# A hybrid streaming encoder step: expert weights through one ring of fourteen half-size slots, with the residual kept on chip and the first projection reordered

## The reference, cut to what matters

```
x = x + gate * mixer(adaLN(rmsnorm(x), c))     # layer 0: GLA + gated DeltaNet heads, layer 1: MLA attention
x = x + gate * moe(adaLN(rmsnorm(x), c))       # both layers
moe(h): 4 groups x 8 experts = 32; a token takes the best group and its 2 best experts
        y = sum of 2 of  w * (silu(h @ w1[e]) * (h @ w3[e])) @ w2[e]     # 1024 -> 512 -> 1024
layer-0 mixer: z = h @ w_in (1024 x 3608); a short convolution, silu and l2norm on q, k; chunked scans; output product
y = rmsnorm(x)
```

## Time and profile before

| what | value |
|---|---|
| median of three runs | 2421.89 us (2415.78 to 2421.91) |
| the profiled execution | 2422.05 us, span of its instructions 2420.2 us |
| mean granted TensorE clock | 0.874 of full speed |
| busy: PE / DVE / ACT / POOL | 79% / 26% / 20% / 5% of the span |
| moved by DMA | 557.66 MB, mean 230 GB/s |
| projection of layer 0 | about 68 to 349 us |
| experts of layer 0 and of layer 1 (routing to last product) | 763 to 1321 us, 1803 to 2362 us |
| combine of layer 0 and of layer 1 | 1338 to 1367 us, 2378 us to the end |

### The profile page before, as it was taken

How to read it: one execution, slowest core, us unless ns; L and a number is a source line. 1 busy time by engine, 2 the same in 40 slices (tenths; PEclk the granted TensorE clock), 3 DMA queues, 4 the chain that set the end, 5 groups by cost and what they waited for, 6 DMA issues and landing times. The chain is left out here.

```text
span 2420.2 us, 29969 instructions
## 1 busy us (share of the span) xinstructions
PE 1900.4 (79%) x12405; PEld 1167.0 (48%) x12405; DVE 633.5 (26%) x1309; ACT 482.2 (20%) x905; POOL 124.3 (5%) x167
## 2 busy tenths in 40 slices
PE   4899937777494889889896189999956989898980
PEld 1899925667484433333332154566953333333420
DVE  1225326334545100100110512333442100010104
ACT  3232262211302000000000341344120000000003
POOL 0000000210000110000000000000001001010000
PEclk7889956798795899999999599999957999999995
DMA  7343380144525399999996720101351999999984
GB/s 292 70 158 132 132 56 5 66 155 144 204 98 187 139 428 385 428 414 401 399 395 284 275 72 3 68 1 36 133 216 60 425 410 406 414 401 405 399 350 176
DMA packets 130328, 557.66 MB, mean 230 GB/s; under 512 B 43432, under 2 KB 76024, under 8 KB 104336
## 3 DMA queue, kind: packets, MB, share of 16 engines
q1 hardware_dynamic: 116176, 535.63, 57.0%
q0 software_dynamic: 11520, 17.85, 2.1%
q10 hardware_dynamic: 2496, 2.23, 0.3%
HBM read 541.65 MB, written 38.12 MB: 240 GB/s over the span
## 5 line engine op out<-in xcount | busy, mean ns | idle before, releaser
L1948 PE MATMUL ex_p<-ring,ex_xT 128*64 128x512 f32 (+1 forms) x1024 | 472.3, 619 | 69.8 <-DMA second<-in_moe_w 67.1
L1948 PE MATMUL ex_p<-second,ex_xT 128*64 128x512 f32 (+1 forms) x1024 | 468.8, 615 | 0.0
L1948 PEld LDWEIGHTS ex_p<-ring,ex_xT 128*64 128x64 f32 (+1 forms) x1024 | 156.4, 156 | 368.0 <-issue 364.5
L2011 DVE TENSOR_TENSOR ex_gm<-ex_s,ex_p 128x512 f32<-128x512 f32 x40 | 27.5, 688 | 891.4 <-issue 859.8
L1964 PE MATMUL ex_py<-ring,ex_gT 128*64 128x512 f32 (+1 forms) x512 | 231.7, 606 | 33.5 <-DMA second<-in_moe_w 17.9
L1964 PE MATMUL ex_py<-second,ex_gT 128*64 128x512 f32 (+1 forms) x512 | 232.1, 607 | 6.3 <-DVE ex_gT L2015 6.3
L1948 PEld LDWEIGHTS ex_p<-second,ex_xT 128*64 128x64 f32 (+1 forms) x1024 | 155.7, 155 | 61.2 <-issue 61.2
L1995 ACT COPY ex_y<-ex_py 128x1024 f32<-128x1024 f32 x40 | 40.5, 1012 | 707.0 <-PE ex_py L1964 707.0
L1964 PEld LDWEIGHTS ex_py<-ring,ex_gT 128*64 128x64 f32 (+1 forms) x512 | 75.4, 152 | 161.2 <-issue 132.8
L230 PE MATMUL ab_z<-ab_hh,ab_wh 128*128 128x288 f32 (+3 forms) x272 | 79.9, 294 | 25.9 <-DVE ab_wl L264 25.9
L230 PE MATMUL out_py<-out_wh,out_oh 128*128 128x256 f32 (+1 forms) x320 | 92.3, 289 | 1.9 <-DVE out_ol L1575 1.8
(11 more groups left out here) (426 smaller groups left out, 3037.2 us busy)
## 6 DMA issues: line engine op xcount, KB each, us to landing
ring<-in_moe_w SPq DMA_DIRECT2D x96, 2048.0 KB, 16.0
second<-in_moe_w SPq DMA_DIRECT2D x96, 2048.0 KB, 18.1
ring<-in_ada_w SPq DMA_DIRECT2D x32, 1536.0 KB, 7.9
ring<-in_ab_w_in SPq DMA_DIRECT2D x7, 2048.0 KB, 7.7
cb_y<-yrow SPq DMA_DIRECT2D x16, 512.0 KB, 9.7
xres<-x SPq DMA_DIRECT2D x12, 512.0 KB, 2.6
mod<-mod SPq DMA_DIRECT2D x12, 512.0 KB, 7.6
x<-xres SPq DMA_DIRECT2D x12, 512.0 KB, 9.7
```

Of the source, the lines that this page charges most:

```text
L1948: last = nc.tensor.matmul(out[r, :], xT[:, b % 2, q, r], wk[:, q, :], start=q == 0, stop=q == KT - 1)
L2011: nc.vector.tensor_tensor(gm[:], s[:], p3[:], ALU.mult).then_inc(gm_ready, 1)
```

## The change

Five parts, in the order of the program.

1. Projection: `ga` and `gb` become a feature-major unit of 8 features, transposed afterwards. GLA's values (ten token-major tiles) move from the start to behind the convolution, and the l2norm's rounds run between them; the output gates come last. The six history stores are issued by ACT between the convolution and the values. Four buffers hold the gates on their way out, two before.
2. Conditioning rows: their store no longer waits within the phase; whoever reuses the buffer or reads later waits on one counter.
3. The residual stays in SBUF from the first output phase to the end; `xres` and its reads and writes are gone. The MoE gate rows load in `phase_route`.
4. Experts: one ring of fourteen slots of 1 MB (six in `ring`, eight in `second`), used strictly in order. Each matrix comes in two halves, and a product releases a slot after each half. Turns are pair, wide, pair, wide, pair. No expert is forced to a place, nothing is loaded ahead: the first fourteen loads start in `phase_route` when `order` is written.
5. The w2 product runs by halves of its inner dimension, both output halves inside.

The core of the diff:

```diff
-def order_of_blocks():
...
-        out += [(5 * g + w, w, w) for w in range(2)]
-        out += [(5 * g + 2 + j, 0, 1) for j in range(3)]
+PATTERN = (2, 1, 2, 1, 2)
+EXPERTS_IN = PATTERN * TURNS
...
+        loads += [(b, k, half, j, n + j) for k in range(3) for half in range(2) for j in range(experts)]
...
-    lead = (NE - 1 - np.arange(NE)) + np.array([1 << 21, 1 << 20] + [0] * (NE - 2))
+    lead = NE - 1 - np.arange(NE)
...
+def load_weights(g, sp, l, rt, second, loads, done=None):
+    weights = (g.io["moe_w1"][l], g.io["moe_w3"][l], g.io["moe_w2"][l])
+    expert = {}
+    for i in loads:
+        b, k, half, j, n = LOADS[i]
+        if n not in expert:
+            expert[n] = sp.value_load(rt.order[0:1, n:n + 1], min_val=0, max_val=NE - 1)
+        if i >= SLOTS:
+            last = LOADS[i - SLOTS]
+            sp.wait_ge(done[last[1]], 2 * last[0] + last[2] + 1)
+        src = weights[k][bass.ds(expert[n], 1)].rearrange("o a n -> (o a) n")
+        src = src.rearrange("(p k) n -> p (k n)", p=P)[:, PIECE * half:PIECE * half + PIECE]
+        sp.dma_start(slot_of(g, second, i), src).then_inc(g.slot_here[i % SLOTS], 16)
...
+            @block.sync                                    # phase_route
+            def _(sp):
+                for c in range(2):
+                    sp.dma_start(gate[:, c, :], bcast_rows(io["mod"][2 * l + 1, c, 2 * D:3 * D])).then_inc(g.gate_here, 16)
+                sp.wait_ge(order_ready, 1)
+                load_weights(g, sp, l, rt, second, range(SLOTS))
...
+                def up(b, out, k, done):                   # phase_experts, PE
+                    for half in range(2):
+                        ws = weights_of(b, k, half, DE)
+                        for q in range(KT // 2):
+                            at = KT // 2 * half + q
+                            for w, r in zip(ws, parts(b)):
+                                last = nc.tensor.matmul(out[r, :], xT[:, b % 2, at, r], w[:, q, :], start=at == 0, stop=at == KT - 1)
+                        last.then_inc(done, 1)
...
-                tm_unit(5, lambda t: zs[0:width(t), t, :], None).then_inc(gab_done, 1)    # projection, PE
+                for t in range(NT):
+                    last = nc.tensor.transpose(zs[0:width(t), t, :], gabT[:, t * P:t * P + width(t)], g.c(K_ID, 2 * NH, 2 * NH))
+                last.then_inc(gab_done, 1)
...
+                for j in range(2 * NT):
+                    tm_tile(10 + j // NT, j)
+                    if 0 < j < 9:
+                        squares_sum(j - 1)
...
-                    sp.wait_ge(hist_done, 12)              # projection, SP
...
+                            act.dma_start(io[name][0, 0, i].rearrange("(f p) -> p f", p=P), hist[:, c, :, i]).then_inc(hist_out, 16)
...
-                for t in range(NT):                        # phase_out, SP
-                    sp.wait_ge(y_ready, (UNITS - 1) * NT + t + 1)
-                    sp.dma_start(io["xres"][s][t * P:t * P + width(t), :], xt[0:width(t), t, :]).then_inc(x_out, 16)
-                sp.wait_ge(x_out, 16 * NT)
```

More of the change, by code:

```diff
@@ L75, with weight_loads @@
 K_END = K_EH + 64
-def order_of_blocks():
-    out = []
-    for g in range(TURNS):
-        out += [(5 * g + w, w, w) for w in range(2)]
-        out += [(5 * g + 2 + j, 0, 1) for j in range(3)]
-    return out
-BLOCKS = order_of_blocks()
+PATTERN = (2, 1, 2, 1, 2)
+EXPERTS_IN = PATTERN * TURNS
+def weight_loads():
+    loads, n = [], 0
+    for b, experts in enumerate(EXPERTS_IN):
+        loads += [(b, k, half, j, n + j) for k in range(3) for half in range(2) for j in range(experts)]
+        n += experts
+    return loads
+LOADS = weight_loads()
 def first_rows():
-    wide = [P * (5 * (r // 2) + r % 2) for r in range(WIDE)]
-    pair = lambda i: 5 * (i // 6) + 2 + i % 6 // 2
-    return wide + [P * pair(i) + P // 2 * (i % 2) for i in range(NE - WIDE)]
+    wide = [P * b for b, experts in enumerate(EXPERTS_IN) if experts == 1]
+    return wide + [P * b + P // 2 * j for b, experts in enumerate(EXPERTS_IN) if experts == 2 for j in range(2)]
 def constants():
@@ L341, in __init__ @@
         self.ps = ctx.enter_context(g.nc.psum_tensor(f"cond_ps_{s}", [3 * STRIP, 512], F32))
[L342 removed]
+        self.mm, self.sum, self.bias_here = (g.semaphore(f"cond{s}_{n}") for n in ("mm", "sum", "bias_here"))
         for i, n in enumerate(self.index):
@@ L979, in _ @@
                                                    ALU.mult, ALU.mult).then_inc(l2_done, 1)
+                    if f == 0:
+                        cond.add(dve, 0)
+                    if f in (4, 7):
+                        split.lo(dve, 12 + f // 7)
+                for u in (14, 15):
+                    split.lo(dve, u)
                 cond.add(dve, 1)
@@ L1936, in take_rows, with parts, weights_of @@
                     last.then_inc(tx_done, 1)
-                def rows(sets):
-                    return [(w, slice(HALFP * j, HALFP * j + HALFP)) for j, w in enumerate(sets)] if len(sets) == 2 else [(sets[0], slice(0, P))]
-                def up(b, sets, at, out, k):
-                    for w, i in zip(sets, at):
-                        pe.wait_ge(here(w, k), landed(w, k, i))
-                    for q in range(KT):
-                        for w, r in rows(sets):
-                            wk = space(w, k).rearrange("p (k n) -> p k n", k=KT)
-                            last = nc.tensor.matmul(out[r, :], xT[:, b % 2, q, r], wk[:, q, :], start=q == 0, stop=q == KT - 1)
-                    return last
+                def parts(b):
+                    return [slice(HALFP * j, HALFP * j + HALFP) for j in range(2)] if EXPERTS_IN[b] == 2 else [slice(0, P)]
+                def weights_of(b, k, half, wide):
+                    found = []
+                    for j in range(EXPERTS_IN[b]):
+                        i = index[b, k, half, j]
+                        pe.wait_ge(g.slot_here[i % SLOTS], slot_landed(l, i))
+                        found.append(slot_of(g, second, i).rearrange("p (k n) -> p k n", n=wide))
+                    return found
+                def up(b, out, k, done):
[6 more added lines that the diff above has]
+                        last.then_inc(done, 1)
                 def gate_transposes(b):
@@ L2146, in phase_combine @@
 @phase
-def phase_combine(g, s, rt, xt, last):
+def phase_combine(g, s, rt, xt, gate, last):
     nc, io = g.nc, g.io
@@ L2154, in phase_combine @@
         y = sb("y", [P, NT, 2, D])
-        gate = sb("gate", [P, 3, D])
+        nw = sb("nw", [P, D]) if last else None
         ss = sb("ss", [P, NT])
@@ L2166, in _ @@
             def _(sp):
-                for c in range(2):
-                    sp.dma_start(gate[:, c, :], bcast_rows(io["mod"][s, c, 2 * D:3 * D])).then_inc(gate_here, 16)
                 for t in range(NT):
```

448 lines of the change are left out of this document (213 added, 235 removed).

## The result

The changed kernel takes 2328.42 us (median of 4 runs, 2321.03 to 2331.42) where the kernel before takes 2421.90 in the same session: ratio 0.9614, 95% interval 0.9584 to 0.9644. The forecast was 2325, in a range of 2280 to 2378. The profiled execution of the changed kernel is its fastest run: its span is 2319.2 us, that of the kernel before 2420.2, so the two traces differ by 101.0 us, 7.5 more than the medians.

The account below looks back on a forecast made before the run. In the experts neither PE nor DMA was busy throughout (too coarse a hand-over); unpaused, DMA would set the phase by a little. Experts -66, projection -20, phase ends -4, combines -4 and -3: -97 from 2422 gives 2325 us, range 2280 to 2378.

Parts of the forecast that it names:

- The experts, -33 per layer: Expert phases: an unpaused weight stream at 420 GB/s moves the phase end from 1321.4 to 1288, -66 for both layers.
- the rival on the other side: Expert weight streams: DMA pays per row, so shorter rows cost +28 us per layer, 2447 in all; chance 0.08.
- the two chains stop each other: Experts: PE's and DMA's sequences of work, ending 9 us apart, stop each other at times; 3 us added, end at 1288.
- The projection, -20: Projection phase: three moves on the path and a store no longer awaited at the end, -20 us, ends -40 to -10.
- (a): Projection, `ga`/`gb` unit: 21.2 us becomes a 6.0 us feature-major tile plus 1 us of transposes, -14.
- (b): Projection, l2norm tail: 40 us goes, 16 come back as ACT sets a 44.6 us loop with the value tiles, -24.
- (c): Projection, history stores moved to ACT's queue: on the path there, +20 us, ends 0 and 27.5.
- Phase ends and combines, -4, -4, -3: Four phase ends without a receipt wait, -4 us; layer 0's combine, -4; last combine, -3.
- PE sets the experts: Experts: half matrices always in time, only PE's 466 us and gaps remain; -44 per layer, 2283 in all; chance 0.12.
- Experts unchanged: Experts: pauses only move elsewhere, leaving the projection and small terms, 2391 in all; chance 0.08.
- Somewhat slower pieces: Experts: stream at 405 GB/s, -18 per layer, with history stores holding ACT 27.5 us; 2365 in all; chance 0.20.
- Smaller rows cost too much: Expert weight streams: a DMA cost per row turns 501 us to 565, +28 per layer, 2447 in all; chance 0.08.

Follow-up runs that it names:

- half the bytes: Changed kernel with half of each weight piece loaded, PE doing the same products, against the changed kernel; one execution: experts' `order` to last copy 497.6 and 496.8 us.
- two pairs at the end: Last turn of each layer ordered wide, pair, wide, pair, pair, against the version with history stores on SP and l2norm in pairs; 2281.56 us, ratio 0.9431.
- wide-first: Changed kernel with the earlier block order (wide, wide, pair, pair, pair per turn) in the ring of fourteen halves; 2351.51 us, ratio 0.9703 to the kernel before.
- whole slots: Changed kernel with seven slots of 2 MB instead of fourteen of 1 MB; 2337.06 us, ratio 0.9643 to the kernel before.

## Why the prediction was right, and where not

*The experts, -33 per layer; measured -29.3 and -27.4.* The rate was better than the 420 that I took (425, worth 6 us of 501), and the smaller rows cost 1%: the rival on the other side had no ground. The fixed cost per transfer of the Trainium skill ("DMA: Bandwidth & Descriptors", section "Anatomy of one DMA — SWDGE (gpsimd) path"), about 2.0 us, did not show in this stream, whose transfers are SP's: at 425 GB/s a 1 MB piece follows the one before it by 2.5 us, where cost and bytes in a row would make it 4.4, an estimate by that section. PE's own chain was well sized (500 us behind `order` forecast, 497 measured with half the bytes). The mis-sized term is the 3 us for "the two chains stop each other": the end stands 17 us behind the 499 that the rate gives, where the sum has 7 (3.9 for half a w2 product, and the 3). Two places are seen for it: the last 15 us of the stream, in which the DMA share falls away, and PE's rest of work behind its last wait at 1213.6, of which two pairs at the end take 2 us at most. How much the uneven end costs by itself stays open. Of what earns the gain the forecast had no picture: by the runs of wide-first and whole slots the interleaved order gives 12 to 14 us of it, the half size 4 to 5; what is left (28.4 on the mean of both layers, less 12.9 and 4.6: some 11, if these add up) would be the rest of the change, the one ring loaded in order of use above all; no run shows it by itself.

*The experts' weights loaded ahead.* I booked them as a loss of the experts alone. They were also a cost of the norm, since SP put them ahead of the row stores. That step failed by leaving out a queue: in the profile 9 us per layer came back there. This hangs on the clock too: without the loads the stage takes 39 us at the full clock but 47.5 at the half, where little more than 1 us is left of it.

*The projection, -20; measured -14.5.* (a) had its price right: the feature-major `ga`, `gb` tile is over in 6 us, its transposes in 0.4. (b) had its loop right: 45.0 us against 44.6. (c) is the mis-sized term: 20 us of stores on ACT, measured 30.4, and 25.4 to 36.7 over eight executions of that phase. The upper end, 27.5, was too low as well: it was SP's time for the same stores in one execution, not a bound. The reason for taking less, that conditioning loads ahead had part of SP's time, is not borne out: on ACT, with no such loads ahead of them, the stores took 25 us or more. With 30.4 the sum would be -10; two things that it left out lie between that and -14.5. From the first copy of q, k to the first of the convolution the trace has 119.7 us with ten value and ten gate tiles before (2.83 us a tile) and 40.4 without them after, some 23 us gained where (a) has 14. And the last conditioning product, which lay beside the l2norm before, now stands alone behind the last gate and puts SP's closing store off by some 3 us:

```profile
324.81 3.69 PE L368 MATMUL cond_ps<-ring,silu 128*32 128x128 f32 x96
```

*Phase ends and combines, -4, -4, -3; measured about -3.5 up to the norm, -5.7 and -6.6.* In the right place; with its receipt waited for, the conditioning store alone costs 4.4 us.

*The latent attention stage, 0; measured +4.6.* Not a cost of the change: over all runs the stage takes 394.9 to 403.8 us, with code that is the same in most. In the changed kernel's profile the granted clock is 0.87 for 40 us at the start of the heads (0.99 before).

*The rivals.* "PE sets the experts" is excluded by 497 against 516. "Experts unchanged" is excluded. "Somewhat slower pieces" is excluded by 425 GB/s where it has 405, and by 28 us per layer where it has 18; of it only the dearer stores came true (27.5, measured 30.4). "Smaller rows cost too much" is excluded by the same rate. So the forecast was right in its main mechanism, an unbroken stream at full rate. That the traces differ by 101 us where it said 97, and the median lies 3 us above it, is luck in part, owed to errors of both signs: +9 in the experts, +6 in the projection, +5 in the attention, -19 in the norms, -5 in the combines.

## What to carry to other kernels

A transfer of many single elements (1536 here) belongs on a queue that nobody waits for; issued by ACT it kept ACT from computing for 30 us. When two engines are near balance, order the work so that its demand for data is even from block to block: that was worth more here than smaller pieces or an earlier start. Before calling an early load free, look at what stands behind it in its queue.

## What was not expected of the hardware

Six stores of 1536 single elements each hold the issuing engine for 25 to 37 us on ACT (eight executions) and 22 to 29 us on SP (six), and for a different time in every execution. The router's products after 13 us of PE idle run at 1.2 GHz to the end of the stretch in some executions (3.47 us for 16) and at 2.4 GHz from soon after their start in others (1.87), with the same instructions and with or without DMA beside them; what decides it the runs do not show. And 1 MB loads in 8 KB rows run at 425 GB/s with fourteen open, 99% of the rate of 2 MB loads.
